# Other SBUF addresses for the low weights, the constants and every activation tile of a two-layer RWKV-7 / sparse-attention trunk

## The reference, cut to what matters

```python
for i in range(DEPTH):                       # DEPTH = 2
    xn = rms_norm(h, mix_norm[i])
    if i % N_MIXERS == 0:
        y, v_raw = rwkv7_time_mix(xn, ...)   # r, k, v projections, low-rank gates, state scan, output projection
    else:
        y = nsa_mix(xn, ...)                 # q, 6 k/v projections, gates; compressed, selected, window attention; output projection
    h = h + y
    h = h + squared_relu_mlp(rms_norm(h, mlp_norm[i]), mlp_w1[i], mlp_w2[i])   # square(relu(x @ w1)) @ w2
```

## Time and profile before

| | |
|---|---|
| median of three runs | 777.41 us (769.6 to 778.11) |
| the profiled execution | 770.58 us |
| its span, first to last instruction | 768.5 us |
| TensorE busy with matmuls / weight loads | 740.7 us / 695.2 us |
| VectorE / ScalarE / GpSimd busy | 520.1 / 379.2 / 70.5 us |
| mean granted TensorE clock | 0.993 of full |
| moved by DMA | 109.24 MB, mean 142 GB/s |

### The profile page before, as it was taken

One profiled execution on the slowest core, in us unless ns is written; L12 is line 12 of the kernel. 1 busy time (PEld: TensorE's weight loads), 2 busy tenths in 40 slices (PEclk: granted clock), 3 DMA queues, 4 the chain that ended last, 5 costly groups with the idle time before them and its releaser, 6 DMA issues.

```text
span 768.5 us, 18778 instructions
## 1 busy us (share of the span) xinstructions
PE 740.7 (96%) x7940; PEld 695.2 (90%) x7940; DVE 520.1 (68%) x742; ACT 379.2 (49%) x584; POOL 70.5 (9%) x50
## 2 busy tenths in 40 slices
PE   7999999998999999999999999988899999999997
PEld 6988888997879999999999989866589999999997
DVE  4896985677453788785555678687858887864441
ACT  6656453211443545544444435668866544543341
POOL 0000005190130000000000010024420000000000
PEclk9999999999999999999999999999999999999999
DMA  9854330000111589967666553500045666676551
GB/s 294 272 174 137 96 101 26 5 3 2 58 57 55 165 233 237 241 191 225 193 197 193 169 165 112 164 1 2 1 147 166 203 196 191 191 218 194 191 165 55
DMA packets 110894, 109.24 MB, mean 142 GB/s; under 512 B 7120, under 2 KB 109776, under 8 KB 110704
## 3 DMA queue, kind: packets, MB, share of 16 engines
q1 hardware_dynamic: 110832, 108.34, 46.9%
HBM read 107.28 MB, written 1.05 MB: 141 GB/s over the span
## 4 chain that ended last, share of the span: by engine, by line
PE 84%; DVE 8%; SPq 2%; ACT 2%; DMA 1%; issue 1%; POOL 1%; ACTq 0%; DVEq 0%; POOLq 0%
PE ps L454 64%; PE ps L670 4%; DMA raw<-in_rwkv_w_in 1%; DVE Gs L1715 1%; DVE SB L2057 1%; PE ps L767 1%; PE ps L982 1%; PE ps L569 1%; PE ps L971 1%; PE ps L1001 1%; PE ps L756 1%; DVE nmx L2063 1%; DVE LT L1741 1%; PE ps L552 1%; POOL t L2126 1%
## 5 line engine op out<-in xcount | busy, mean ns | idle before, releaser
L1530 DVE TENSOR_TENSOR wlo<-raw,whi 128x1024 fp32r<-128x1024 f32 x188 | 226.1, 1225 | 88.8 <-ACT whi L1124 86.5
L1124 ACT ACTIVATE whi<-raw 128x1024 fp32r<-128x1024 f32 x124 | 130.3, 1058 | 128.1 <-PE ps L454 122.4
L454 PE MATMUL ps<-xh,whi 128*128 128x256 f32 x896 | 178.1, 280 | 2.7 <-DVE wlo L1530 1.1
L454 PE MATMUL ps<-xl,whi 128*128 128x256 f32 x896 | 175.4, 277 | 0.0
L454 PE MATMUL ps<-xh,wlo 128*128 128x256 f32 x896 | 175.2, 277 | 0.0
L454 PEld LDWEIGHTS ps<-xh,whi 128*128 128x128 f32 x896 | 135.4, 188 | 6.8 <-issue 4.3
L454 PEld LDWEIGHTS ps<-xl,whi 128*128 128x128 f32 x896 | 135.5, 188 | 0.0
L454 PEld LDWEIGHTS ps<-xh,wlo 128*128 128x128 f32 x896 | 135.4, 188 | 0.0
L1359 ACT ACTIVATE whi<-raw 128x1024 fp32r<-128x1024 f32 x64 | 68.0, 1063 | 78.0 <-PE ps L454 59.2
L454 PE MATMUL ps<-hl,whi 128*128 128x256 f32 x512 | 99.8, 276 | 0.0
L454 PE MATMUL ps<-hh,whi 128*128 128x256 f32 x512 | 99.6, 276 | 0.0
(11 more groups left out here) (308 smaller groups left out, 974.6 us busy)
## 6 DMA issues: line engine op xcount, KB each, us to landing
raw<-in_mlp_w SPq DMA_DIRECT2D x128, 512.0 KB, 4.5
raw<-in_rwkv_w_in SPq DMA_DIRECT2D x24, 512.0 KB, 5.1
raw<-in_nsa_w_in SPq DMA_DIRECT2D x20, 512.0 KB, 4.7
raw<-in_rwkv_w_out SPq DMA_DIRECT2D x8, 512.0 KB, 3.4
raw<-in_nsa_w_out SPq DMA_DIRECT2D x8, 512.0 KB, 3.5
cw<-in_nsa_cmp_w SPq DMA_DIRECT2D x4, 512.0 KB, 9.1
cst<-in_consts SPq DMA_DIRECT2D x1, 1047.0 KB, 11.3
xtok<-in_x SPq DMA_DIRECT2D x2, 512.0 KB, 4.2
```

The source lines that it names most:

```text
L454: last = mm(ps[:, bank0 + m, 0:T], w[:, slot, c0:c0 + P], x_[:, kk, :], start=(kk == 0 and n == 0), stop=(kk == ktiles - 1 and n == 2))
L1124: A(whi[:, s, :], raw[:, s, :], ACT.Copy).then_inc(hi_ready, 1)
L1530: v.tensor_tensor(wlo[:, slot, :], raw[:, slot, :], whi[:, slot, :].bitcast(f32), ALU.subtract)\
```

## The change

`wlo` moves up by 64 bytes, and with it `cst`, `par`, `tiny`, `rs` and `ri`. `blk` is then put at 96 modulo 128, which is 160 bytes above its old place, and all tiles in the 16 blocks and in `misc` go with it. `h`, `raw` and `whi` stay. Modulo 128, `wlo` is at 64 after the change, `xh`, `xl`, `yh`, `yl`, `hh`, `hl` and the others of the blocks at 96. No instruction, wait, order, shape or size differs.

```diff
     whi = place("whi", [P, RING, UE], dt=r32)
+    base[0] += 64
     wlo = place("wlo", [P, RING, UE], dt=r32)
...
-    blk = base[0]
+    blk = (base[0] + 127) // 128 * 128 + 96
     off = lambda n, b=0: blk + n * BLK + b
```

## The result

The changed kernel takes 791.28 us, median of four runs (789.8 to 794.53); the kernel before, with one more run, 777.76 us (769.6 to 779.48). The quotient of these medians is 1.017; the ratio on record, worked out from the single runs, is 1.023, 95% interval 1.018 to 1.028. It is slower, by more than the runs of before spread; whether by more than 2% these runs leave open. Beside the 13 runs of before taken with the first experiments (median 770.94 us) it would be 2.6%. The profiled execution took 789.8 us, span 787.8, 19.3 us more than the traced one of before.

A forecast was written before the change was run, and what follows sets the result against it. It took TensorE's large products, 4512 times their pace, plus a few stages of short steps between engines, as the bound. Its terms summed to 0 against the profiled 770.58 us, giving 771 us, range 752 to 786.

The forecast's parts named there:

- I take 0 between these ends: Large products on TensorE: the new addresses change their pace by nothing, between a 16.2 us loss and a 21.3 us gain.
- the level turns within a stage at the same addresses: Products near 264 us: pace goes from 117.5 to 113.8 ns with addresses modulo 128 unchanged, so start-up selects the level.
- the exchange of roles: Large products with inputs standing and weights moving: 113.3 ns over 21 steps, read as exchanging the two phases does nothing.
- a third level: Sign of a wrong prediction: large products at a pace other than the two levels, 113.3 and 117.8 ns.
- different paces for high and low weights: Sign of a wrong prediction: large products with high and low weights, now at different distances, differ in pace.
- means of VectorE or GpSimd off by over 2%: Sign of a wrong prediction: these engines' mean times in the scan and attention move by over 2%.
- The upper bound: Large products: all at the slow level, 3672 paying 4.4 ns each, 16.2 us more, ending at 786.8 us.
- Rival C: Large products: the new distance holds them at the slow level, 117.8 ns in the MLPs; 787 us, chance 0.19.
- Rival B: Large products: the distance counts and the new one is cheaper; 758 us, from 749 to 767, chance 0.38.
- VectorE, ScalarE, DMA: Work outside the large products: the moved addresses cost or save 0 on each of these.
- The reading of 777 us: Spread of the runs before: higher runs have one MLP block of 1536 products at the slow level, adding 6.8 us.
- the lower bound: Large products: all 4512 at 109.4 ns, the pace of turning tiles at line 612, saving 21.3 us, to 749.3 us.

The follow-up runs named there:

- the first experiments: The follow-up runs taken first; the 13 runs of the unchanged kernel before taken with them had a median of 770.94 us.
- b2: The kernel before with no edit, traced once more (first of two further traces): 770.25 us.
- b3: The kernel before with no edit, traced once more (second of two further traces): 772.77 us.
- the series: Kernels of their own with only rows of products, operand places varied, some with other widths, engine traffic or fp32; fp32r with 256 columns took 113.3 to 129.7 ns.
- e2: Against the kernel before, only the blocks (inputs) moved, to 96 modulo 128, wlo staying at 0: 798.85 us, ratio 1.036.
- e3: Against the kernel before, every tensor moved up by 32 bytes, distances unchanged: 771.52 us, ratio 0.999.
- e4: Against the kernel before, the blocks moved to 0 modulo 128, so inputs and both weights stand at distance 0: 795.63 us, ratio 1.030.
- e6: Against the kernel before, weights stay and the blocks' data moves to 112 modulo 128 (240 modulo 256): 770.8 us, ratio 0.995.

## Why the prediction was wrong

It forecast 771 us and no change, with 752 to 786; 791.3 came. The step that failed is the one on the large products, "I take 0 between these ends". It rested on two readings. That the level turns within a stage at the same addresses is true, and b2 and b3 confirm it; but it shows only that two levels are open at the distance of before, not that the distance doesn't decide which are open. At 96/32 the traces show one level, 118.3. And the exchange of roles in the earlier trace rows was no test: it turns 64 into -64, which modulo 128 is the same distance, as the text itself said; modulo 256 it is 192 and 64, at which the series show the same two levels. Nor was the reading complete. The earlier trace rows shows the first of four such units; the next one, in the same trace of before, has 22 steps in 2.59 us, 117.7 ns, and the last two go so as well:

```profile
497.12 0.28 PE L952 MATMUL ps<-wlo,xh 128*128 128x256 f32 x1
...
499.71 0.28 PE L953 MATMUL ps<-whi,xl 128*128 128x256 f32 x1
```

The term was not 0 but 5.0 ns a product in the MLPs, 15.1 us there; that the distance makes it is shown by e2, e3, e4 and e6. The prediction's own sign of being wrong, a third level, is what came; the other two, different paces for high and low weights and means of VectorE or GpSimd off by over 2%, did not (GpSimd is busy 70.4 us, before 70.5).

- *The upper bound* was no bound. "All at the slow level", 786.8, took the slowest level of the trace for the slowest there is. The changed kernel stands at 118.3, e2 and e4 at 120.0 throughout with medians up to 799 us, one row of a series at 129.7.
- *Rival C* named the right place (the MLPs, from 265 us on) and nearly the right price, 16.2 us against 19.3. It was the sign that would show it: 117.8 or more from 265 to 439 us. It was given 0.19. Its mechanism, that the row stays at the old slow level, was off: it is a level of its own. That its price came near is luck in part, as 118.3 happens to lie by 117.8; at e2's distances the traced time rose by 28.6 us.
- *Rival B*, that a distance can be cheaper, is borne out in part by e6, for another distance and for 0.2 to 0.5% rather than 1.5: the slow level is gone from its MLPs and projections, but a pace under 113.3 ns was not seen with 256 columns. What it says of the load holds in the trace of before: at line 454 a weight load starts 3 ns after a product does and takes 188 ns (medians).
- *VectorE, ScalarE, DMA* at 0: right. `wlo` kept 1225 ns, the reduction 1220 and the mask 1222.
- *The reading of 777 us* as one MLP block at 117.8 ns stays open: three traces of before and one of e3 show both MLPs at 113.3. That e6, at whose distance the series show the quick level alone, has no such run speaks for it.

For fp32r, places alone moved the pace of a product of 256 columns between 113.3 and 129.7 ns; for fp32 they moved nothing, 215.8 ns a recorded matmul at every distance tried. The 109.4 ns of the earlier trace rows, on which the lower bound and the aim of rival B rest, no series of 256 columns reached.

What inside the chip makes the pace hang on the places was not tried and stays open. Shown is that it hangs on the distance of the moving operand from the stationary one (113.3 to 129.7 ns), at distance 112 on a step of 32 bytes (113.5 to 114.2 ns on it, 118.3 to 120.0 off it), on the width of the load (distance 112 at 113.9 ns with 128 columns, at 120.0 with 64 in two rows of three), and at some distances on something that differs from row to row at the same addresses (113.5 and 117.8 ns for (0,0,192)). That the period is 256 bytes rests on one distance, 368, which goes as 112 does.

## What to carry to other kernels

Where a row of fp32r products with a fresh load each bounds a kernel, treat the distance between the two operands' starts as a parameter and measure it: here the worst place tried cost 3.6% against that of before, with not one instruction changed. An unchanged pace under an exchange of roles proves nothing about the distance, and a stretch that shows two levels at one set of addresses does not show that addresses are idle. Before a placing is taken over, look at the pace from start to start over a thousand products, not at the recorded durations (276 ns for `hh` in the earlier trace rows, at a pace of 113.4): a series of its own gave within 0.1 ns what the kernels do at distances 0, 96 and 96/32, but at 64/0 it missed 1.1 ns of one MLP. And print the addresses after a change of placing: 16 bytes more in one tensor moved the next by 64.

## What the hardware showed that was not expected

- A shift of both operands by 32 bytes is free (771.52 against 770.94 us), by 16 it is not (at distance 112, from 113.9 to 118.3 and 120.0 ns).
- Distance 0, both on full 128-byte steps, is among the dearest: 120.0 ns.
- With 128 moving columns the place is without effect at the four distances tried, 111 to 112 ns a product wherever the clock was full.
